# A skip term folded into a convolution kernel, and a carry readout interleaved with a gate product: one transformer-like block on one Trainium2 core

## The reference, cut to what matters

```
h = modulate(x, g_mix, sh1, sc1)            # rms_norm * (1 + scale) + shift, from c @ w_ada
proj = h @ w_in                             # 256 tokens x (512 + 1024 + 2048)
u_a, z_b, gate_logits = split(proj)         # z_b = gelu(...)
y = u_a * s5_d                              # the skip term, one factor per channel
for direction in (forward, backward):       # state-space scan over context, then tokens
    h_re, h_im = s5_scan(u, ab, bb, s0=state after the context)
    y = y + s5_readout(h_re, h_im, c_re, c_im)
y = gelu(y);  y_a = y * sigmoid(y @ w_glu + b_glu)
y_b = sgu_mixer(z_b, ...)
g_a, g_b = split(sigmoid(gate_logits + b_gate))
x = x + ga1 * ((g_a * (y_a @ w_proj_a) + g_b * (y_b @ w_proj_b)) @ w_out)
x = x + ga2 * conv_ffn(modulate(x, ...))    # up product, 3x3 depthwise conv, silu gate, down product
return rms_norm(x, g_final)
```

## Time and profile before

| what | value |
|---|---|
| median of 3 runs | 472.12 us (471.29 to 472.27) |
| the profiled execution's own time | 472.59 us |
| its span in the profile | 470.8 us |
| TensorE busy | 455.9 us, 97% of the span |
| VectorE busy | 403.5 us, 86% |
| ScalarE busy | 105.9 us, 22% |
| chain that ended last, by engine | TensorE 77%, VectorE 16%, DMA 3% |
| mean granted TensorE clock | 0.985 |

### The profile page before, as it was taken

The page is one execution under the profiler, slowest core; times in us unless marked ns, Lnnn a source line. Parts: engine busy times, 40 slices in busy tenths (PEclk is TensorE's granted clock), DMA queues, the critical chain, the costliest instruction groups (busy, mean ns, idle before and its releaser), DMA issues.

```text
span 470.8 us, 7801 instructions
## 1 busy us (share of the span) xinstructions
PE 455.9 (97%) x2671; PEld 351.1 (75%) x2671; DVE 403.5 (86%) x836; ACT 105.9 (22%) x198; POOL 48.1 (10%) x77
## 2 busy tenths in 40 slices
PE   8899999989999899999989999999999999999994
PEld 5677857888888788885468888887888887444454
DVE  4598999999999867789755999998999999899644
ACT  5423355135104005201161111011011111200002
POOL 2001100003013232100000111010011011000000
PEclk9899999999999969999999999999999999999999
DMA  8994499633999999993986543452443443000002
GB/s 296 419 419 144 130 340 170 223 144 81 111 274 402 411 397 399 402 412 135 427 318 253 179 166 116 166 180 94 173 178 112 155 178 137 41 0 1 0 1 89
DMA packets 22091, 97.41 MB, mean 207 GB/s; under 512 B 6504, under 2 KB 7152, under 8 KB 13360
## 3 DMA queue, kind: packets, MB, share of 16 engines
q1 hardware_dynamic: 15024, 74.70, 44.0%
q0 software_dynamic: 5632, 20.71, 13.8%
q10 hardware_dynamic: 1408, 1.63, 1.0%
HBM read 94.44 MB, written 2.59 MB: 206 GB/s over the span
## 4 chain that ended last, share of the span: by engine, by line
PE 77%; DVE 16%; DMA 3%; issue 2%; ACT 1%; SPq 0%; DVEq 0%; ACTq 0%
PE bank L764 31%; PE bank L775 14%; PE bank L565 11%; DVE s_region L1043 8%; PE bank L672 6%; PE bank L716 4%; PE bank L480 4%; DMA gates<-early_w 3%; PE bank L653 2%; PE bank L693 1%; DVE s_region L1162 1%; PE bank L445 1%; DVE s_region L1300 1%; DVE gates L1043 1%; DVE s_region L1331 1%
## 5 line engine op out<-in xcount | busy, mean ns | idle before, releaser
L764 PE MATMUL bank<-h_all,s_region 128*128 128x256 f32 x704 | 152.6, 379 | 0.9 <-ACT ctx_region L992 0.7
L764 PEld LDWEIGHTS bank<-h_all,s_region 128*128 128x128 f32 x704 | 133.1, 190 | 20.2 <-ACT ctx_region L992 1.1
L1571 DVE SCALAR_TENSOR_TENSOR ctx_region<-ctx_region,pk_sb 128x189 f32<-128x189 f32 (+2 forms) x352 | 127.5, 439 | 0.2 <-DVE ctx_region L1571 0.2
L565 PE MATMUL bank<-h_all,ring_region 128*128 128x256 f32 x256 | 58.2, 389 | 0.5 <-DVE s_region L1331 0.5
L565 PEld LDWEIGHTS bank<-h_all,ring_region 128*128 128x128 f32 x256 | 49.8, 196 | 8.3 <-DVE s_region L1331 0.7
L775 PE MATMUL bank<-s_region,ring_region 128*128 128x512 f32 (+1 forms) x132 | 47.6, 521 | 0.0
L775 PEld LDWEIGHTS bank<-s_region,ring_region 128*128 128x128 f32 x132 | 25.1, 190 | 22.6 <-issue 21.5
L992 ACT ACTIVATE ctx_region<-bank 128x512 f32<-128x512 f32 x22 | 13.2, 599 | 126.1 <-PE bank L764 69.7
L1043 DVE TENSOR_TENSOR s_region<-s_region,power 128x2048 f32<-128x2048 f32 (+1 forms) x16 | 38.1, 2421 | 0.2
L397 POOL TENSOR_TENSOR ring_region<-gates,ctx_region 128x256 f32 x22 | 17.3, 785 | 181.2 <-ACT gates L997 181.2
L1561 DVE TENSOR_SCALAR ctx_region<-ctx_region,pk_sb 128x256 f32<-128x256 f32 x44 | 21.1, 522 | 13.2 <-ACT ctx_region L992 12.1
(11 more groups left out here) (241 smaller groups left out, 518.0 us busy)
## 6 DMA issues: line engine op xcount, KB each, us to landing
s_region<-up_w SPq DMA_DIRECT2D x33, 1024.0 KB, 4.8
ring_region<-ring_w SPq DMA_DIRECT2D x22, 1024.0 KB, 9.0
s_region<-mod_w POOLq DMA_DIRECT2D x22, 512.0 KB, 13.9
s_region<-early_w SPq DMA_DIRECT2D x4, 1024.0 KB, 21.8
s_region<-out_w SPq DMA_DIRECT2D x4, 1024.0 KB, 12.7
h_all<-mod_w POOLq DMA_DIRECT2D x6, 512.0 KB, 16.6
gates<-early_w SPq DMA_DIRECT2D x2, 1024.0 KB, 10.8
s_region<-k_scratch POOLq DMA_DIRECT2D x8, 256.0 KB, 12.0
```

Of the source, the lines that this page charges most:

```text
L565: mx = pe.matmul(bank[5 - j % 2][:, mm * TOK:(mm + 1) * TOK], ring[:, u % RING, (mm * KD + k) * P:(mm * KD + k + 1) * P], h_x[:, k, :], st ...
L764: mx = pe.matmul(bank[s % 3][:, half * TOK:(half + 1) * TOK], up_ring[:, s, (half * KD + k) * P:(half * KD + k + 1) * P], h2[:, k, :], sta ...
L1571: dve.scalar_tensor_tensor(out=o, in0=a, scalar=cw[:, tile[half], (dy + 1) * 3 + dx + 1], in1=o, op0=ALU.mult, op1=ALU.add).then_inc(s_con ...
```

## The change

- The skip term is added to lag 0 of the Toeplitz kernel. The packed parameters get an identity of 16 columns per group (`eye_h`); VectorE multiplies it by `s5_d` into `skip_eye` and adds it to `k_lag0`, between its copies of jobs 5 and 7. The store of `k_sb` waits for that (`s_k_skip`), and ScalarE copies job 6 ahead of the store. The copy of u to `u_x` (`L1261`) and the eight skip operations (`L1425`) go.
- The gelu reads the two PSUM banks of the transposes directly, one activation for each bank.
- The carry readout is cut into four parts (bank, direction), and between them and behind the last stand the four quarters of gate unit 7 (one output tile, half of k). ScalarE copies bank 0 as soon as its two parts are done.
- The transpose of ga1 moves from ahead of the GLU product to behind projection (3,0), and ScalarE's copy and store of it behind the GLU's sigmoids.
- VectorE's merge takes both gate products in one operation of 512 columns.

```diff
+        skip_eye = a_raw[:, 0:KS * H].rearrange("p (m h) -> p m h", m=KS)
+        k_lag0 = k_sb.rearrange("p (m j h) -> p m j h", m=KS, j=LAGS)[:, :, T - 1, :]
...
 # TensorE
-            pe.wait_ge(s_scan, 1)
-            for g2 in range(2):
-                half = slice(g2 * N, (g2 + 1) * N)
-                for d, r, e0 in ((0, 0, 1), (0, 1, 1), (1, 0, 0), (1, 1, 0)):
+            def carried(g2, d):
+                half = slice(g2 * N, (g2 + 1) * N)
+                for r in range(2):
                     for j in range(P // H // 2):
                         for m in range(KS):
                             q = m * (P // H // 2) + j
                             mx = pe.matmul(bank[g2][m * CH:(m + 1) * CH, j * P:(j + 1) * P], carry[half, (r * 2 + d) * PAIRS + q, :],
-                                           ca[half, d, r, q, e0:e0 + T, :].rearrange("p e h -> p (e h)"),
+                                           ca[half, d, r, q, 1 - d:1 - d + T, :].rearrange("p e h -> p (e h)"),
                                            start=False, stop=(d == 1 and r == 1), skip_group_check=True)
-                mx.then_inc(s_y8_ps, 1)
-            gate_unit(7)
+                if d == 1:
+                    mx.then_inc(s_y8_ps, 1)
+            def last_gate_part(mm, k0):
+                u = U_GATE + GATES - 1
+                for k in range(k0, k0 + KD // 2):
+                    mx = pe.matmul(bank[4][:, mm * TOK:(mm + 1) * TOK], ring[:, u % RING, (mm * KD + k) * P:(mm * KD + k + 1) * P],
+                                   h_x[:, k, :], start=(k == 0), stop=(k == KD - 1))
+                if mm == 1 and k0 > 0:
+                    mx.then_inc(s_unit, 1)
+            pe.wait_ge(s_scan, 1)
+            carried(0, 0)
+            ring_ready(pe, U_GATE + GATES - 1)
+            pe.wait_ge(s_gate, 2 * (GATES - 2))
+            last_gate_part(0, 0)
+            carried(0, 1)
+            last_gate_part(0, KD // 2)
+            carried(1, 0)
+            last_gate_part(1, 0)
+            carried(1, 1)
+            last_gate_part(1, KD // 2)
...
-            pe.wait_ge(s_ga1, 1)
-            pe.transpose(bank[3][0:KD, 0:P], mod2[:, 0:KD], ident[:, :]).then_inc(s_ga1_tr, 1)
             ring_ready(pe, U_GLU)
-            pe.wait_ge(s_ygelu, 1)
+            pe.wait_ge(s_ygelu, 2)
...
-            pe.wait_ge(s_y, 2 * KS)
             projection(3, 0)
+            pe.wait_ge(s_ga1, 1)
+            pe.transpose(bank[3][0:KD, 0:P], mod2[:, 0:KD], ident[:, :]).then_inc(s_ga1_tr, 1)
             pe.wait_ge(s_ya, KS)
...
 # ScalarE
-            act.wait_ge(s_k, 2)
+            chunk_inputs_copied(6)
+            act.wait_ge(s_k_skip, 1)
             act.dma_start(k_dram[:].rearrange("m p n -> p m n"), k_sb[:, :].rearrange("p (m n) -> p m n", m=KS)).then_inc(s_k_out, 16)
-            chunk_inputs_copied(6)
...
-            act.wait_ge(s_y8_ps, 2)
             for b in range(2):
+                act.wait_ge(s_y8_ps, b + 1)
...
-            act.wait_ge(s_y, 2 * KS)
-            act.activation(y_gelu.rearrange("p m (c t) -> p m t c", t=T), y_feat, ACT.Gelu_apprx_tanh).then_inc(s_ygelu, 1)
+            for b in range(2):
+                act.wait_ge(s_y_tr, b + 1)
+                act.activation(y_gelu.rearrange("p m (c t) -> p t m c", t=T)[:, 4 * b:4 * b + 4],
+                               bank[b][:, :].rearrange("p (t m c) -> p t m c", t=4, m=KS), ACT.Gelu_apprx_tanh).then_inc(s_ygelu, 1)
...
 # VectorE
-            dve.wait_ge(s_uf, KS)
-            dve.tensor_copy(u_x[:, :]..., u_feat...).then_inc(s_ux, 1)
+            dve.wait_ge(s_pk2, 16)
+            tt(skip_eye, par("eye_h").unsqueeze(1).broadcast_to([P, KS, H]), par("s5_d").unsqueeze(2).broadcast_to([P, KS, H]), ALU.mult)
...
             for job in (3, 4, 5, 7):
+                if job == 7:
+                    dve.wait_ge(s_k, 2)
+                    dve.tensor_tensor(k_lag0, k_lag0, skip_eye, ALU.add).then_inc(s_k_skip, 1)
...
-            dve.wait_ge(s_pk2, 16)
-            for b in range(2):
-                dve.wait_ge(s_y_tr, b + 1)
-                ... 4 scalar_tensor_tensor (u_x * s5_d + bank) each -> y_feat
             modulation_sums(12, 18)
...
-                tt(t[0], src[:, 0:TOK], gates[:, m, :], ALU.mult)
-                tt(t[1], src[:, TOK:2 * TOK], gates[:, KD + m, :], ALU.mult)
-                settle()
-                dve.tensor_tensor(merged[:, m, :], t[0], t[1], ALU.add).then_inc(s_mg, 1)
+                tt(merge_tmp, src[:, :].rearrange("p (b t) -> p b t", b=2), gates[:, m:m + KD + 1:KD, :], ALU.mult)
+                settle()
+                dve.tensor_tensor(merged[:, m, :], merge_tmp[:, 0, :], merge_tmp[:, 1, :], ALU.add).then_inc(s_mg, 1)
```

More of the change, by code:

```diff
@@ L72 @@
 for _name, _w in [("c", KD), ("c_ctx", KD), ("b_ada", NMOD * KD), ("g_mix", KD), ("pick", 2), ("g_ffn", KD),
-                  ("b_gate", 2 * KD), ("b_glu", KS), ("s5_d", KS), ("conv_b", 2 * KF), ("conv_w", 2 * KF * 9)]:
+                  ("b_gate", 2 * KD), ("b_glu", KS), ("s5_d", KS), ("conv_b", 2 * KF), ("conv_w", 2 * KF * 9), ("eye_h", H)]:
     _PK[_name] = (_at, _at + _w)
@@ L116, in build @@
         y_tok = ctx_region[:, 0:1024]
-        y_feat = ctx_region[:, 1024:2048].rearrange("p (m t c) -> p m t c", m=KS, t=T)
         glu_gate = ctx_region[:, 0:1024].rearrange("p (m t) -> p m t", m=KS)
@@ L236, in build @@
         s_wsrc, s_tr, s_win = sem("w_src_ready"), sem("transposed"), sem("w_in_evacuated")
-        s_ux = sem("u_x_copied")
         s_bpad, s_ca = sem("b_pad_ready"), sem("ca_ready")
@@ L243, in build @@
         s_sgu_ps, s_yb = sem("sgu_in_psum"), sem("y_b_ready")
-        s_k_ps, s_k, s_k_out, s_m = sem("k_in_psum"), sem("k_evacuated"), sem("k_stored"), sem("m_loaded")
+        s_k_ps, s_k, s_k_skip, s_k_out, s_m = sem("k_in_psum"), sem("k_evacuated"), sem("skip_added_to_k"), sem("k_stored"), sem("m_loaded")
         s_e_ps, s_e, s_ev, s_scan = sem("e_in_psum"), sem("e_evacuated_by_act"), sem("e_evacuated_by_dve"), sem("carry_ready")
@@ L248, in build @@
         s_y8_ps, s_y8, s_y_tr = sem("y_by_chunk_in_psum"), sem("y_by_chunk_ready"), sem("y_transposed")
-        s_y, s_ygelu = sem("y_with_skip_ready"), sem("y_gelu_ready")
+        s_ygelu = sem("y_gelu_ready")
         s_glu_ps, s_glu, s_ya = sem("glu_in_psum"), sem("glu_gate_ready"), sem("y_a_ready")
@@ L886, in gate_sigmoids @@
                                    ACT.Sigmoid, bias=par("b_gate")[:, m:m + 1]).then_inc(s_gate, 1)
-            act.wait_ge(s_ux, 1)
+            act.wait_ge(s_u_out, 16 * KS)
             act.wait_ge(s_pk2, 16)
@@ L949, in last_rows @@
                 act.activation(rows1[:, n % 2, :], bank[LATER_BANK[n]][:, 2 * P:4 * P], ACT.Copy).then_inc(s_rows, 1)
+            act.wait_ge(s_ga1_tr, 1)
+            act.activation(ga1_rows, bank[3][0:KD, 0:P], ACT.Copy).then_inc(s_ga1_sb, 1)
+            act.wait_ge(s_ga1_sb, 1)
+            act.dma_start(ga1_dram[:].rearrange("a (k p) -> (a k) p", p=P), ga1_rows).then_inc(s_ga1_out, 16)
             preload_sqrt()
@@ L1258, in _ @@
                         mark(ins)
-            dve.wait_ge(s_uf, KS)
-            dve.tensor_copy(u_x[:, :].rearrange("p (m c) -> p m c", c=CH), u_feat.rearrange("p m t c -> p (m t) c")[:, :, CH:2 * CH]).then_inc(s_ux, 1)
+            dve.wait_ge(s_pk2, 16)
+            tt(skip_eye, par("eye_h").unsqueeze(1).broadcast_to([P, KS, H]), par("s5_d").unsqueeze(2).broadcast_to([P, KS, H]), ALU.mult)
             for r in range(2):
@@ L1442, in _ @@
                 src = bank[PROJ_BANK[m % 4]]
-                t = merge_tmp[:, 0, :], merge_tmp[:, 1, :]
-                tt(t[0], src[:, 0:TOK], gates[:, m, :], ALU.mult)
-                tt(t[1], src[:, TOK:2 * TOK], gates[:, KD + m, :], ALU.mult)
+                tt(merge_tmp, src[:, :].rearrange("p (b t) -> p b t", b=2), gates[:, m:m + KD + 1:KD, :], ALU.mult)
                 settle()
-                dve.tensor_tensor(merged[:, m, :], t[0], t[1], ALU.add).then_inc(s_mg, 1)
+                dve.tensor_tensor(merged[:, m, :], merge_tmp[:, 0, :], merge_tmp[:, 1, :], ALU.add).then_inc(s_mg, 1)
                 dve.wait_ge(s_mg, m + 1)
@@ L1732 @@
     pk = np.concatenate(_features(a["c"][0], a["c_ctx"], a["b_ada"][0], a["g_mix"][0]) + [pick]
-                        + _features(a["g_ffn"][0], a["b_gate"][0], a["s5_b_glu"][0], a["s5_d"][0], a["conv_b"][0]) + [conv_w], axis=1)
+                        + _features(a["g_ffn"][0], a["b_gate"][0], a["s5_b_glu"][0], a["s5_d"][0], a["conv_b"][0]) + [conv_w, np.tile(np.eye(H, dtype=np.float32), (P // H, 1))], axis=1)
     def per_state(v):
```

## The result

| | before | changed |
|---|---|---|
| median | 471.71 us | 478.65 us (477.05 to 483.06, 4 runs) |
| ratio to before | | 1.0155, 95% interval 1.0115 to 1.0195 |
| profiled execution, its span | 472.59, 470.8 us | 479.42, 477.6 us |

A forecast was written before the change was run, and what follows sets the result against it. TensorE bounds 150 to 214 us; the readout's gain was to be lost waiting for late tiles. 472.59 + 3.4 (later resumption) + 2.0 (lower clock) = 478.0, median 0.47 below: 477.5 us, range 468 to 480.

The forecast's parts named there:

- Readout and gate unit 7: TensorE: gap and clock drop go, so the stretch takes 13.7 us in place of 20.97, 7.3 less.
- VectorE's chain: VectorE, 44 to 113 us: the copy of u goes, a small product comes; gate unit 1 starts 0.54 us earlier.
- The k store: Toeplitz kernel store waits for the skip, issued about 113.0, not 110.10; all GpSimd's loads come 2.9 us later.
- The bursts: SP's 2 MB transfers slow the modulation tiles: the first holds them back 5.5 us, the second up to 5.5 more.
- Tile 17: Modulation tile before y_a: lands between 190.7 and 196.2, middle 193.5 taken; TensorE resumes at 196.3, +3.4 us.
- The clock behind the stop: After about 11 us idle, TensorE resumes dense work at the lower clock: +2.0 us.
- The sum: Whole kernel: 472.59 + 3.4 + 2.0 = 478.0, with the runs' median 0.47 lower: 477.5 us.
- (a): Rival: modulation tiles not late, TensorE never waits, whole gain kept: 464.3 us; chance 0.15.
- (b): Rival: only part of the tiles' delay comes true, tile 17 between 186 and 190.7: about 470 to 474.7; chance 0.20.
- (c): Rival: the readout's gap and lower clock stay, only 0.54 us is won: 471.6 us; chance 0.10.
- the loss of 3.9: Whole kernel's loss if DMA queues take packet turns, read as equal shares: 3.9 us in place of 5.4.
- 3.3 us for the second burst: SP's second burst before tile 17: by the packet-turn rule it adds 3.3 us at most in place of 5.5.

The follow-up runs named there:

- e3: Changed kernel with the carry readout in one piece again and gate unit 7 behind it: 477.73 us, ratio 1.0134 to the kernel before.
- f2: Kernel before, with only ScalarE's Toeplitz kernel store held until VectorE has copied jobs 3, 4 and 5: 478.48 us, ratio 1.0132.
- f5: Kernel before, with only the modulation sums spread: y_a behind sum 14, one or two sums behind each merge, 24 to 27 behind the last: 475.79 us, ratio 1.0071.
- g2: g1 with the carry readout in one piece ahead of gate unit 7: 474.08 us, ratio 1.0048 to the kernel before.
- f1: Kernel before, with only the readout in four parts between gate unit 7's quarters and ScalarE's early bank copies: 472.23 us, ratio 0.9993.
- e2: Changed kernel with the skip added to lag 0 before VectorE's copy of job 3: 473.89 us, ratio 1.0032 to the kernel before.
- g1: Changed kernel with skip added ahead of job 3, y_a behind sum 14, later sums spread behind the merges: 468.76 us, ratio 0.9933 to the kernel before.
- g4: g1 with the skip added between jobs 5 and 7 again, so the store is late: 473.58 us, ratio 1.0039 to the kernel before.
- e4: Changed kernel with the last two output-weight units issued behind ring units 21 and 22, not 19 and 20: 480.27 us, ratio 1.0174 to before.

## Why the prediction was right, step by step

- **Readout and gate unit 7.** Gap and clock drop gone, as taken; that rested on the guess that the gap is code arriving late, which no run proves. The size was 15.2 us (four parts of 1.88 and four gate quarters of 1.92) in place of 13.7: each change between small and large products costs some 0.2. A stop of 1.1 us came on top, which I had not seen: gate unit 7 waits for sigmoid 5, which stands on ScalarE behind c's row, itself behind the late loads. Gate unit 7 ended at 171.9 in place of 170.3. Every profile with the readout in one piece that I compared (before, e3, f2, f5, g2) has the gap, 2.0 to 2.3 us, and none of the interleaved ones has it.
- **VectorE's chain.** Gate unit 1 started 1.4 us earlier, not 0.54. But in f5, with VectorE's work there as before, it started 0.5 later, and f1's store went out 1.2 earlier: executions differ by that much.
- **The k store: the term that was mis-sized.** I charged 2.9 us for all of GpSimd's loads. The store was issued at 111.95, 1.85 later than before (forecast 113.0), took 4.57 us to land in place of 3.06, and the loads ended 7.8 later (147.03 against 139.22), since the lateness grows where they meet SP's ring units. For the tiles it is 4.3 (tile 9), in place of 2.9. f2 shows that a late store alone costs 6.2 us of time.
- **The bursts: about right.** I charged 5.5 us to the first and 2.8, half as much, to the second, 8.3 in all. Measured from tile 9 to tile 17 are 19.4 - 10.8 = 8.6. One burst alone was 4.8 to 5.0 (f1, e2, e3, f2).
- **Tile 17** came at 195.2, inside 190.7 to 196.2 and 1.7 after the 193.5 taken: 1.4 of that is the store's and 0.3 the bursts'. That the middle of the range was so good a choice is luck, since nothing in the rows told how much of the second burst falls ahead of tile 17. TensorE resumed at 197.82 (forecast 196.3).
- **The clock behind the stop.** 22.61 - 20.72 = 1.9 us, forecast 2.0.
- **The sum.** 197.82 - 192.87 = 4.9, and 1.9, make 6.8: the difference of the spans, 477.6 - 470.8. Forecast 5.4.
- **Rivals.** (a), no tile late, is what the reordered g1 comes near (468.8, not 464.3). (b), part of the delay, is what e2 makes of it (473.9). (c), the gap stays, did not come true. By the Trainium skill (Runtime: NRT & Kernel Launch, Instruction fetch mechanics) code fetching is hidden. The runs here speak against it without proving it: the gap went with a change of order alone, and a packet of the queue of kind instruction started at 160.56 and took 1.1 us, so it was in 1.4 us before TensorE resumed at 163.09. In the other four profiles with the gap TensorE resumed 1.2 to 1.4 us behind the end of such a packet as well, and behind the 1.24 us gap near 104 us of before it is 1.3. The line of the DMA view of before, 160.4 to 160.6 us:

```profile
q8 instruction: 1, 0.02, 34.0%
```

By the Trainium skill (DMA: Bandwidth & Descriptors, Queues, rings and completion order) each DMA engine takes turns between its queues packet by packet. The trace agrees, but turns are not equal shares of the bytes, which is how I used the rule. The DMA view of the changed kernel from 178.6 to 182.4 us, under a burst (queue, packets, MB, share; q1 carries SP's transfers, q0 GpSimd's):

```profile
q1 hardware_dynamic: 146, 1.07, 67.3%
q0 software_dynamic: 145, 0.53, 34.9%
```

As many packets each, but SP's are twice as large. A third of the engines makes 3 x 1.28 = 3.84 us of a tile, and tiles 10 and 11 landed 3.75 apart. The 2.56 us and the loss of 3.9 that I took for the rule's are those of equal bytes; nor do the rows give its 3.3 us for the second burst (8.6 x (1 - 1.28/2.56) is 4.3).

Shown by runs: the late store costs 5.0 to 6.2 us by the ratios in each of three settings (f2 against before, changed against e2, g4 against g1); the interleaving is worth 5.4 us in g1 against g2 and nothing in the medians of the changed kernel (e3) and of before (f1). In the changed kernel that is the stop in front of y_a; in f1 the traced execution did gain 3.9, and what the others lost is not shown. Open: why f1 spreads over 4 us, and why a late store takes longer to land.

## What to carry to other kernels

Before making an operation wait for one more thing, follow the queue behind it to its last entry: here a store that left 2 to 3 us later, with 8.8 us of cover at its own consumer, put back the loading of 28 weight tiles and cost 5 to 6 us two stages on. A faster engine gains only up to its next operand, and it frees buffers earlier, so its loads compete with the operand it will wait for; check the order of the engine that makes the operand before counting the gain. In a stretch with the DMAs full, an early start is worth more than its length.

## What the runs showed of the hardware that was not expected

- Under full DMA queues a lateness is not carried along one to one: 3.4 us at the issue of the eight 256 KB loads became 7.8 at their end, since they land 2.2 to 2.8 us apart alone and 3.4 to 5.1 beside a ring unit; ten tiles later it was 4.3.
- Two busy queues moved the same number of packets (146 and 145 in 3.8 us), so the one with packets of twice the size took 67% of the engines' time.
- A ring unit of 1 MB issued at about 120 us behind the eight loads landed 17.8 us later (before). From 120.7 to 130 its queue moved 3 packets, the loads' 307; the byte rate was 111 GB/s.
- TensorE's granted clock stayed at 1.00 over stops of 1.0 us (f1), 1.24 (before), 1.7 (f2) and 2.1 (e4, before the Toeplitz product) and was at 0.50 behind stops of 3.2 (e3), 4.5 (e2) and 10.9 us and behind the readout's gap of 2.10; each drop behind a stop cost 1.9 to 2.8 us of dense products.
